# Products without a reader on TensorE, an earlier branch product and a closer split of the channel sums in a two-block kernel on one core

## The reference, cut to what matters

```
def conv_mixers(h, ...):                      # layer 0 of the second block
    gate_b, gate_c, x_a, val_b, glu_gate = split_cols(h @ w_in, AB_SIZES)
    y_a = gate_b * causal_depthwise_conv_2(gate_c * x_a, conv_a)             # 3 taps
    u = causal_depthwise_conv_2(val_b * sigmoid(glu_gate), conv_b) + bias    # 31 taps
    y_b = silu(layernorm(u, ln_g, ln_b))
    return concatenate([y_a, y_b]) @ w_out

for i in range(2):                            # second block
    h = modulate(rmsnorm(x), sh1, sc1)
    y = conv_mixers(h) if i == 0 else attn_mixers(h)
    x = x + g1 * y
    h = modulate(rmsnorm(x), sh2, sc2)
    x = x + g2 * hier_moe(h)                  # 32 experts, top 2, each 1024 x 512 x 1024
```

## Time and profile before

| | |
|---|---|
| device time, 3 runs | 2001.15, 2002.57 (median), 2003.13 us |
| the profiled execution | 2000.23 us, of which the span of the trace is 1998.5 us |
| PE busy | 1945.2 us (97% of the span) |
| DVE, ACT, POOL busy | 1027.9, 369.7, 122.8 us |
| DMA | 593.14 MB, mean 297 GB/s |
| convolution layer | 740 to 849 us; experts of layer 0 to 1332 us |
| attention layer | 1340 to 1512 us; experts of layer 1 to the end |

### The profile page before, as it was taken

The page is one execution under the profiler, slowest core; times in us unless marked ns, Lnnn a source line. Parts: engine busy times, 40 slices in busy tenths (PEclk is TensorE's granted clock), DMA queues, the critical chain, the costliest instruction groups (busy, mean ns, idle before and its releaser), DMA issues.

```text
span 1998.5 us, 21703 instructions
## 1 busy us (share of the span) xinstructions
PE 1945.2 (97%) x8110; PEld 1074.1 (54%) x8110; DVE 1027.9 (51%) x1945; ACT 369.7 (18%) x775; POOL 122.8 (6%) x217
## 2 busy tenths in 40 slices
PE   8999999999999999899999999989999999999997
PEld 5557666545676658554444344447765444344442
DVE  3456875445586759776678686752544011011102
ACT  2421001033100010131111111111332211111111
POOL 1122210011121100000000000000000000000000
PEclk9999999999999999989999999999999999999999
DMA  7437876334587851659999999993254999999995
GB/s 264 156 127 256 297 290 256 141 126 169 180 291 287 304 211 43 256 231 410 426 428 428 425 427 427 427 352 127 85 205 193 407 428 427 426 428 426 426 427 233
DMA packets 113351, 593.14 MB, mean 297 GB/s; under 512 B 17767, under 2 KB 22374, under 8 KB 85990
## 3 DMA queue, kind: packets, MB, share of 16 engines
q1 hardware_dynamic: 99430, 541.48, 67.5%
q0 software_dynamic: 13824, 50.34, 7.1%
HBM read 590.74 MB, written 1.05 MB: 296 GB/s over the span
## 4 chain that ended last, share of the span: by engine, by line
PE 86%; DVE 8%; issue 2%; DMA 1%; POOL 1%; ACT 1%; DVEq 0%; SPq 0%; POOLq 0%; ACTq 0%
PE bank L1251 28%; PE bank L897 11%; PE bank L910 10%; PE bank L1124 6%; PE bank L829 6%; PE bank L1226 5%; PE bank L1242 4%; DVE work L2692 3%; PE bank L1034 3%; PE bank L1144 2%; PE bank L943 1%; PE bank L1398 1%; DMA ring<-in_moe_w_up 1%; PE bank L1234 1%; POOL rstd L749 1%
## 5 line engine op out<-in xcount | busy, mean ns | idle before, releaser
L1251 PE MATMUL bank<-ring,work 128*64 128x512 f32 x2240 | 632.7, 593 | 1.5 <-DMA ring<-in_moe_w_up 1.4
L1251 PEld LDWEIGHTS bank<-ring,work 128*64 128x64 f32 x2240 | 202.1, 137 | 311.5 <-issue 311.3
L2692 DVE SCALAR_TENSOR_TENSOR work<-work 128x512 f32<-128x512 f32 x384 | 262.0, 746 | 6.7 <-DVE work L2690 5.3
L897 PE MATMUL bank<-hT,ring 128*128 128x256 f32 x1024 | 225.1, 379 | 0.7 <-ACT hT L1555 0.7
L897 PEld LDWEIGHTS bank<-hT,ring 128*128 128x128 f32 x1024 | 194.4, 190 | 36.9 <-issue 11.7
L2702 DVE SCALAR_TENSOR_TENSOR work<-work,bank 128x512 f32<-128x512 f32 x32 | 21.9, 686 | 353.7 <-ACT work L1760 353.7
L1251 PE MATMUL bank<-seventh,work 128*64 128x512 f32 x384 | 169.1, 593 | 0.0
L1251 PE MATMUL bank<-work 128*64 128x512 f32 x312 | 140.3, 594 | 0.0
L1124 PE MATMUL bank<-hT,ring 128*128 128x256 f32 x608 | 138.3, 389 | 0.4 <-ACT hT L1670 0.4
L829 PE MATMUL bank<-ring,hT 128*128 128x512 f32 (+1 forms) x320 | 135.0, 579 | 0.0
L1124 PEld LDWEIGHTS bank<-hT,ring 128*128 128x128 f32 x608 | 118.1, 196 | 19.8 <-issue 3.2
(11 more groups left out here) (410 smaller groups left out, 2068.8 us busy)
## 6 DMA issues: line engine op xcount, KB each, us to landing
ring<-in_moe_w_gate SPq DMA_DIRECT2D x51, 2048.0 KB, 16.5
ring<-in_moe_w_down SPq DMA_DIRECT2D x44, 2048.0 KB, 19.6
ring<-in_moe_w_up SPq DMA_DIRECT2D x43, 2048.0 KB, 18.6
ring<-in_w_down SPq DMA_DIRECT2D x16, 2048.0 KB, 11.8
ring<-in_w_up SPq DMA_DIRECT2D x16, 2048.0 KB, 11.6
xn<-in_ada_w POOLq DMA_DIRECT2D x48, 512.0 KB, 6.4
work<-in_ada_w POOLq DMA_DIRECT2D x48, 512.0 KB, 7.4
ring<-in_w_in SPq DMA_DIRECT2D x10, 2048.0 KB, 8.0
```

Of the source, the lines that this page charges most:

```text
L897: last = pe.matmul(b[:, (c % 2) * S:(c % 2) * S + S], w[:, k, c * P:c * P + P], hT[:, k, :], start=(k == 0), stop=(k == DT - 1))
L1251: last = pe.matmul(b[h, :], x[:, k, h], rows_of(i, j + e, k)[:, c0:c0 + 512], start=(k == 0), stop=(k == kk - 1))
L2692: mo.do(dve.scalar_tensor_tensor(fl(bias[:, h]), mask_b, rbt[:, bass.ds(12 * bk + h, 1)], fl(bias[:, h]), ALU.mult, ALU.add))
```

## The change

The change has four parts.

1. A helper `unread(dst, n)` issues n matmuls whose result nobody reads: `ones` as the stationary operand, `ident` as the moving one, into a place that is written again or free. It stands in `norm2(0)` ahead of tile 1 (6 of 128 columns), in `norm2(2)` ahead of tile 0 (10) and tile 1 (4), in the convolution layer ahead of the wait for `y_ready` 2 (2 of 512 columns), and in the attention tail between `mixed(2)` and `mixed(3)` (2 of 512 columns, after a wait until `gate1b` is drained).
2. DVE's product for `y_a` moves three taps forward, six instructions, from behind tap 24 to behind tap 21.
3. In the convolution layer two of the four matmuls between `ln_mu` and `ln_var` move behind `ln_var`, and ACT's table load stands before the wait for `ln_mu`.
4. In the head of the experts, in both layers, two of the four clears move behind the rank products.

```
+UNREAD_TURNS = {(0, 1): 6, (2, 0): 10, (2, 1): 4}
...
+            def unread(dst, n):
+
+                for _ in range(n):
+                    pe.matmul(dst.rearrange("p (a n) -> p a n", n=P), ones[:, :], spread(ident[:, :], 1, dst.shape[1] // P), start=True, stop=True,
+                              skip_group_check=True)
+
             def norm2(nth):
 
                 for t in range(TT):
+                    if (nth, t) in UNREAD_TURNS:
+                        unread(B(4)[:, t * P:t * P + P], UNREAD_TURNS[nth, t])
                     pe.wait_ge(s2["xd_act" if t == 0 else "xd_dve"], nth // 2 + 1)
                     turn(t, lambda c: xn[:, t, c * P:c * P + P])
...
             over_channels("ln_mu", "u_ready", abx[3])
-            out_part(0, AB_OUT, 6, landed2, mixT, ROW1[:1])
+            out_part(0, AB_OUT, 6, landed2, mixT, ROW1[:1], 0, 2)
             over_channels("ln_var", "uq_ready", abx[4])
+            out_part(0, AB_OUT, 6, landed2, mixT, ROW1[:1], 2, 4)
             out_part(0, AB_OUT, 6, landed2, mixT, ROW1[1:])
+            unread(B(OWN_BANK["ln_mu"]), 2)
             pe.wait_ge(s2["y_ready"], 2)
...
                 pe.wait_ge(m["exp_in"], 2 * i + 1)
-                clear((0, 1, 2))
+                clear((0,))
                 pe.wait_ge(m["sel_ready"], i + 1)
...
                 pe.matmul(B(5)[:, NE:2 * NE], earlier[:, :], sel_e[:, 1, :], start=False, stop=True).then_inc(m["rank_ps"], 1)
+                clear((1, 2))
                 pe.wait_ge(s2["gate_row_drained"], i + 1)
...
             mixed(2)
+            drained2("gate1b")
+            unread(B(OWN_BANK["gate1a"]), 2)
             mixed(3)
...
+            act.activation(orec[:, 0:1], lnsq, ACT.Sqrt)
             act.wait_ge(s2["job_filled"], JOB2["ln_mu"] + 1)
             stand(act, s2["job_drained"])
-            act.activation(orec[:, 0:1], lnsq, ACT.Sqrt)
...
-            conv_b(high, 16, 25)
+            conv_b(high, 16, 22)
             drained("ab9")
             dve.tensor_tensor(mixT[:, 0:4, :], abx[1][:, :, :], abx[0][:, :, :], ALU.mult).then_inc(s2["y_ready"], 1)
 
-            conv_b(high, 25, 30)
+            conv_b(high, 22, 30)
             conv_end(high)
```

## The result

The changed kernel takes 1988.02 us (median of 4 runs, 1985.89 to 1989.18) against 2002.59 us (4 runs, 2001.15 to 2003.13): a ratio of 0.9927, 95% interval 0.991 to 0.9944, 14.6 us. The forecast was 1991.0, range 1986 to 1997, faster with 0.92. The profiled execution is 1988.53 us, its span 1986.8.

The account below looks back on a forecast made before the run. TensorE, busy 97% of the span, was taken as the bound, with waits and half-clock stretches to win. Terms 3.9 + 1.7 + 1.9 + 2.2 + 1.7 + 0.9 = 12.3 us off 2000.2, plus 2.3 offset and 0.8 reserve, gave 1991; range 1986 to 1997.

Parts of the forecast that it names:

- the convolution: Convolution layer: earlier `y_a`, closer sums and the first norm's 0.5 us start unit 1 3.9 us earlier; ends 2.7 and 4.9.
- the norm ahead of attention: Norm ahead of attention: with its waits filled, the second transposes and the products behind run at full clock; 2.2 us.
- the tail: Attention tail: two unread products fill a 2.00 us wait; the 32 products take 13.9 instead of 15.60; 1.7 us.
- The start of unit 0: Convolution layer: with `y_a` ready earlier, PE starts unit 0 at 812.8 instead of 816.01; 3.2 us.
- head of layer 0: Experts' head, layer 0: counts 1.7 us earlier with two clears less before them, gather 1.9 us shorter at full clock.
- The term of 1.7: Experts' head, layer 0: two clears less before the counts, so the first two end at 862.9 instead of 864.6; lower end 0.
- head of layer 1: Experts' head, layer 1: the same move of clears, where the fall may only move; 0.9 us, ends 0 and 1.9.
- held back 0.8: Whole kernel: 0.8 us reserve because half-clock stretches will not all lie alike in every execution; 1990.2 became 1991.
- A: Both norms: the clock falls despite the fill, because transposes do not help it; 9.6 us gained, 1993.7; chance 0.17.
- B: Whole kernel: fill does not hold the clock, only order counts (convolution, layer 0's head); 5.1 us gained, 1997.5; chance 0.10.
- C: All fills: they run at 1.2 GHz and overrun their waits; 4.0 us slower, 2006.6; chance 0.03.
- D: Convolution: another input holds the sums or `y_a`, fill and moved falls eat the rest; within 0.2%, 2001; chance 0.05.

Follow-up runs that it names:

- e5_heads_old: The changed kernel with all four clears ahead of the rank products again, in both heads of the experts: 1994.09 us.
- e4_turn_fill: The changed kernel with transposes of the identity in place of both norms' unread products, at the same count of instructions: 1989.01 us.
- e6_no_norm_fill: The changed kernel without the unread products in both norms, those of the convolution and the tail kept: 1990.21 us.
- e10_narrow_fill: The changed kernel with both norms' unread products 8 columns wide instead of 128, at the same count: 1991.36 us.
- e7_tap_old: `e3_no_conv_fill` with the product for `y_a` again behind tap 24 instead of tap 21: 1991.70 us.
- e8_split_old: `e3_no_conv_fill` with four matmuls between the two sums again and the table load behind the wait for the first sum: 1990.92 us.
- e1_order_only: The changed kernel with no unread product at all; the earlier `y_a`, closer sums and moved clears stay: 1988.93 us.
- e11_wide_router: `e3_no_conv_fill` with the router's instructions alone made 108 columns wide instead of 36, at the same count: 1987.92 us.
- e9_wide_both: `e3_no_conv_fill` with the router's instructions widened from 36 to 108 columns and the attention gates' from 8 to 128: 1984.27 us.
- e3_no_conv_fill: The changed kernel without the two unread products ahead of unit 1 of the convolution: 1987.15 us.
- e12_wide_and_head: `e9_wide_both` plus unread products of 1.3 us in the wait before the counts, in both heads of the experts: 1983.58 us.

## Why the prediction was right, and where it was off

**Right: what bounds it, and the parts.** The clock fell behind waits of PE and the fill kept it: 1.00 at 740, around 1330 and at 1487. The stage terms held within 0.2 us for the convolution (4.05 for 3.9), the norm ahead of attention (2.01 for 2.2) and the tail (1.70 for 1.7). That the stages add up to 13.05 us for 12.3 is partly luck, since the two heads missed in opposite directions. The start of unit 0 (3.3 for 3.2), the root (5.05 for 5.0) and the fill ending 1.0 us after `y_b` came as worked out. The loads of the experts moved with PE: the first load that had waited for a free slot is issued at 873.12 instead of 880.68 (SP L609), and the stage takes 462.09 us as before (462.21).

**Mis-sized: head of layer 0.** 1.7 + 1.9 were forecast, 4.86 us seen. The gather gave 1.63 of it. The rest, 3.2, lies between the first logits product and the counts, 12.19 us before and 8.97 after. Without a fall there the counts come after 8.97 us with four clears too (`e5_heads_old`), so in this pair the moved clears gave nothing ahead of the counts, and the whole 3.2 is the fall at 855.5, which in the profiled execution after did not come. I had given the change no part in that, and `e5_heads_old` shows that it is not the moved clears that removed it: this is luck of the executions. The term of 1.7 is right where a fall does stand there (10.54 us with four clears, 8.97 with two, as shown above), and its lower end, 0, was right here. In other executions of the change it may come: it stood there in `e4_turn_fill`, `e6_no_norm_fill` and `e10_narrow_fill`.

**Mis-sized: head of layer 1.** 0.9 was taken between 0 and 1.9; 0.31 came. The gather gained 1.6 as in layer 0 (from its start to the next product 3.76 instead of 5.39 us), but a fall stood ahead of it at 1506.5 to 1514, and from the first logits product to the counts it took 10.48 us instead of 9.04. I wrote that the fall may only move, and in this execution it did.

**The step that failed: from one execution to the medians.** The sum was made on one execution, 2.3 us below its median. I added this offset back as if it were the same for both kernels, and held back 0.8 for falls that might lie elsewhere. Together they are 3.1 us, about the 3.0 from 1991.0 to 1988.0. In fact the profiled execution after lies 0.5 us above its median: 13.05 us of stages, less 1.35 in the first block, plus 2.36 and 0.51 for where the two executions lie beside their medians, are the 14.57 measured. That 14.6 is 12.3 and just the offset is chance, since these parts were not forecast one by one.

The likely seat of the difference is that the two waits of the convolution were priced at their length. In the profiled execution the clock stayed up through the waits of 3.28 and 2.27 us, so closing them was worth 2.7 and what the sums gave. `e7_tap_old` and `e8_split_old` show both waits with a fall behind them, 1.7 us each, in their profiles and in their medians (4.5 and 3.8 us for the two parts, 8.3 together, where the stage gave 5.1 in the profiled pair, the 1.0 that the fill cost included). That the kernel before has these falls in its other executions is inferred, not shown: none of those was profiled, and the mean granted clocks, given to 0.001, do not settle it. Over its runs beside the experiments they are 0.988 to 0.992; 0.991 or more have only four runs, all under 2000.2 us, but the profiled one has 0.990, as the slow ones have. The wait in `e7_tap_old` is also longer, 3.91 us, than the 3.28 of the kernel before, since the first norm's fill brings PE there earlier.

**The rivals.** A (too thin, or transposes do not count) fell by the clock in both norms and by `e4_turn_fill`. B (only the order counts) has the medians almost on its side, 13.0 of 14.6 us with the order alone, but it priced the order at 5.1 and gave another reason: the fill does hold the clock, and what it wins against `e1_order_only` (1.2 us up to unit 0, 1.6 in the norm, 1.7 in the tail) is partly spent, 1.0 in the convolution and 1.4 on a fall that stands in the head of layer 1 (10.48 against 9.05 us to the counts). C happened only in the narrow fill. D did not.

**Open.** Why a fall behind a given wait comes in one execution and not in another was not settled; each kernel was profiled once, so that `e7_tap_old` and `e8_split_old` have a fall behind their waits rests on one trace each and on their medians. The same wait of 1.6 us before the counts shows a fall behind it in `e11_wide_router` and none in the change, layer 0. How much of the 3.7 us between the medians of `e9_wide_both` and `e11_wide_router` belongs to the wide gates is open for the same reason. The fill of the tail was not taken away alone.

## What to carry to other kernels

On an engine that is busy 97% of the time, a wait can cost more than it shows, its own length and 1.7 us of slow work behind it (4.5 us for 2.7, 3.8 for 1.7 here), so first close waits by moving real work into them or the awaited result forward (13.0 of 14.6 us here), and fill only what is left. A fill must end before what it waits beside and be of a kind that a profile shows to keep the clock; where one hole is filled, look at the next wait and at the next run of narrow products, since the fall tends to move there, and count as done only a profile without a stretch at 0.50. One profiled execution shows one draw of the falls: set the sum against the median and ask of each wait which the change closes whether it carries a fall in others.

## What the runs showed of the hardware that was not expected

- Float32 transposes of 128 x 128 hold TensorE's clock at 1.00 in a wait (`e4_turn_fill`, 1327.5 to 1335.5), matmuls of 8 columns in the same number do not (`e10_narrow_fill`, 0.54 at 1328.5 to 1336).
- An instruction of 108 columns takes what one of 36 does: the router's 32 are 3.76 us at full clock as before when 24 of them have 108 columns and 4 have 72. In three kernels so widened no fall stood between these products and the counts (0 of 6 heads, against 14 of 22 with narrow ones); in two of them it came at the next wait.
- Behind a single wait of 2.27 us among dense work of 512 columns a fall came in `e8_split_old` (833 to 837), behind the same wait in the kernel before none, and behind one of 0.55 us in the same place none either (`e3_no_conv_fill`).
- Where the falls are gone the spread between executions is small: 0.4 us from the lowest to the highest of `e12_wide_and_head`, 3.3 for the changed kernel (4 runs each); of `e9_wide_both` the slowest, 1985.61, has a mean granted clock of 0.996 and the other four 0.998 or 0.999.
